# Half of the k tiles of the gate and up products as seven products of sums, four of them in turn in one bank

## The reference

```python
m = rms_norm(h, ffn_norm_g)
return h + (jax.nn.silu(m @ w_gate) * (m @ w_up)) @ w_down
```

## Time and profile before

| what | value |
|---|---|
| time, median of 3 | 2576.79 us (2575.72 to 2576.93) |
| the profiled execution's own time | 2576.22 us |
| its span | 2574.4 us |
| TensorE busy | 2561.0 us (99%) |
| VectorE, ScalarE, GpSimd busy | 1603.7, 1473.3, 824.6 us |
| granted TensorE clock | 1.00 |
| read from HBM | 487.38 MB |

### The profile page before, as it was taken

One profiled execution on the slowest core, in us unless ns is written; L12 is line 12 of the kernel. 1 busy time (PEld: TensorE's weight loads), 2 busy tenths in 40 slices (PEclk: granted clock), 3 DMA queues, 4 the chain that ended last, 5 costly groups with the idle time before them and its releaser, 6 DMA issues.

```text
span 2574.4 us, 30659 instructions
## 1 busy us (share of the span) xinstructions
PE 2561.0 (99%) x11740; PEld 2122.9 (82%) x11740; DVE 1603.7 (62%) x1799; ACT 1473.3 (57%) x1811; POOL 824.6 (32%) x368
## 2 busy tenths in 40 slices
PE   9999999999999999999999999999999999999999
PEld 7888888888887888888888888888878888888887
DVE  6798955434347878787533467456477878786222
ACT  7776645445455656566544575565565656566333
POOL 2687753344441000000444455333320000003443
PEclk9999999999999999999999999999999999999999
DMA  8766654466666475656566644554557565655554
GB/s 302 222 209 204 178 192 161 162 223 210 204 203 246 168 250 174 243 184 217 190 215 205 223 168 157 172 196 142 185 194 247 174 243 183 234 194 194 202 203 147
DMA packets 174705, 516.13 MB, mean 200 GB/s; under 512 B 108027, under 2 KB 111068, under 8 KB 117216
## 3 DMA queue, kind: packets, MB, share of 16 engines
q1 hardware_dynamic: 174128, 513.64, 59.9%
q10 hardware_dynamic: 432, 0.52, 0.1%
HBM read 487.38 MB, written 2.10 MB: 190 GB/s over the span
## 4 chain that ended last, share of the span: by engine, by line
PE 94%; DVE 2%; issue 1%; ACT 1%; POOL 1%; DMA 0%; SPq 0%; ACTq 0%; DVEq 0%; POOLq 0%
PE PB L858 18%; PE PB L862 18%; PE PB L859 18%; PE PB L925 8%; PE PB L926 8%; PE PB L929 8%; PE PB L909 2%; PE PB L906 2%; PE PB L904 2%; ACT WH L1460 1%; PE PB L1168 1%; PE PB L1010 0%; DVE WL L2251 0%; PE PB L1040 0%; POOL WL L3321 0%
## 5 line engine op out<-in xcount | busy, mean ns | idle before, releaser
L3321 POOL TENSOR_TENSOR WL<-RAW,WH 128x1024 fp32r<-128x1024 f32 x280 | 703.1, 2512 | 1730.0 <-ACT WH L1460 1729.1
L1460 ACT ACTIVATE WH<-RAW 128x1024 fp32r<-128x1024 f32 x738 | 776.2, 1057 | 797.6 <-PE PB L862 634.3
L2251 DVE TENSOR_TENSOR WL<-RAW,WH 128x1024 fp32r<-128x1024 f32 x456 | 613.6, 1348 | 753.6 <-ACT WH L1460 752.3
L858 PE MATMUL PB<-WH,HNH 128*128 128x512 f32 x1152 | 458.6, 398 | 2.6 <-ACT TM L2036 2.4
L862 PE MATMUL PB<-WL,HNH 128*128 128x512 f32 x1152 | 449.4, 390 | 1.5 <-POOL WL L3321 1.5
L859 PE MATMUL PB<-WH,HNL 128*128 128x512 f32 x1152 | 448.6, 389 | 0.0
L858 PE MATMUL PB<-WH,HDH 128*128 128x512 f32 x704 | 273.9, 389 | 0.0
L859 PE MATMUL PB<-WH,HDL 128*128 128x512 f32 x704 | 273.9, 389 | 0.0
L862 PE MATMUL PB<-WL,HDH 128*128 128x512 f32 x704 | 273.9, 389 | 0.0
L858 PEld LDWEIGHTS PB<-WH,HNH 128*128 128x128 f32 x1152 | 216.4, 188 | 50.5 <-ACT TM L2036 3.2
L862 PEld LDWEIGHTS PB<-WL,HNH 128*128 128x128 f32 x1152 | 216.2, 188 | 49.0 <-POOL WL L3321 3.4
(11 more groups left out here) (450 smaller groups left out, 3887.0 us busy)
## 6 DMA issues: line engine op xcount, KB each, us to landing
RAW<-in_w_gu SPq DMA_DIRECT2D x136, 1024.0 KB, 7.2
RAW<-in_w_dn SPq DMA_DIRECT2D x88, 1024.0 KB, 4.8
RAW<-in_w_in_a SPq DMA_DIRECT2D x53, 1024.0 KB, 5.2
RAW<-in_w_in SPq DMA_DIRECT2D x45, 1024.0 KB, 4.8
RAWX<-in_w_gu SPq DMA_DIRECT2D x40, 1024.0 KB, 6.6
RAW<-in_w_out SPq DMA_DIRECT2D x32, 1024.0 KB, 4.7
RAW<-in_w_ga SPq DMA_DIRECT2D x24, 1024.0 KB, 4.8
RAW<-in_w_gb SPq DMA_DIRECT2D x24, 1024.0 KB, 4.8
```

The source lines that it names most:

```text
L858: e.matmul(o, hi[:, k, x], WH[:, s, c], start=k == 0, stop=False)
L1460: e.activation(wh(key), source(key), ACT.Copy).then_inc(*wt.act.mark(("wh", *key)))
L2251: e.tensor_tensor(to, raw, hi, ALU.subtract).then_inc(*wt.dve.mark(("wl", *key)))
L3321: e.tensor_tensor(to, raw, hi, ALU.subtract).then_inc(*wt.pool.mark(("wl", *key)))
```

## The change

- Quarters 0 and 1 of the k tiles are done as seven products of sums in all groups 1 to 10, quarters 2 and 3 plainly. A group has 7 x 2 x 2 x 3 = 84 and 96 matmuls, 180 in all.
- A unit of weights is now a key pair (block, c), c being one of its halves, in the order b11, b22, t1, t2, b21, t3, up 2, t4, gate 2, gate 3, up 3.
- Four blocks (b11, t2, t3, t4) and the second token half of the gate columns are summed in one bank x. ScalarE copies what x holds after b11, t2 and t3 (`part`, at k == 10, 36, 53), and t1 from bank z (k == 28). A block that goes on in x waits for the copy. Odd and even groups use two sets of four banks.
- The first sum, t1 = gate 0 + up 0, is made by a DMA issued by GpSimd that reads gate 0 from HBM again and adds it into the buffer that holds up 0 (`first_sum`). It waits for the load of up 0. The sums t2, t3 and t4 stay with VectorE, now for both halves.
- There are five buffers for loads in the gate and up part. To make room, X (2 MB) is stored to HBM early in group 0 and brought back (`x_back`) at the start of the down products.
- The loads of a group come in the order up 0, gate 0, up 1, gate 1, up 2, gate 2, gate 3, up 3.

```diff
-BLOCKS = ("b11", "b21", "b22", "t1", "t2", "t3", "t4")
-BANK_OF = (1, 2, 3, 5, 6, 7, 4)
-SUMMED = (1,)
-FIRST_PLAIN = 0
-SUM_BEHIND = {0: 3, 2: 4, 3: 5, 4: 6}
-STARTS = {(32 * i + 6) // 7: i for i in range(7)}
+BLOCKS = ("b11", "b22", "t1", "t2", "b21", "t3", "t4")
+BANK_OF = {"b11": "x", "b22": "y", "t1": "z", "t2": "x", "b21": "w", "t3": "x", "t4": "x"}
+SUM_BEHIND = {("b22", 1): (("t2", 0),), ("t1", 0): (("t2", 1),), ("t1", 1): (("t3", 0),), ("t2", 0): (("t3", 1),),
+              ("b21", 0): (("t4", 0),), ("b21", 1): (("t4", 1),)}
...
+        AWAY = nc.dram_tensor("away", (128, 2, 2048), F32).ap()
...
+        RAWX = [ar(f"RAWX{i}", [128, RU * 128], 16 + 8 * i) for i in range(2)]
+        WX = [at(f"WX{i}", [128, 2, SU * 128], F32R, (arena + 32 * KB, xt_off, xt_off + 8 * KB)[i]) for i in range(MORE)]
+        CP = ar("CP", [128, 2, 512], 40)
...
+        items = [(b, c) for b in BLOCKS[:6] for c in range(2)] + [(("up", 2), c) for c in range(2)]
+        items += [("t4", c) for c in range(2)] + [((of, d), c) for of, d in (("gate", 2), ("gate", 3), ("up", 3)) for c in range(2)]
+        takes = [6 if b in BLOCKS else 12 for b, c in items]
+        starts = [-(-128 * sum(takes[:i]) // sum(takes)) for i in range(len(items))]
+        place_in_group = [("up", 0), ("gate", 0), ("up", 1), ("gate", 1), ("up", 2), ("gate", 2), ("gate", 3), ("up", 3)]
...
+            if place >= NRAW and raw_before[n] < n - 50:
+                first_in_raw[n] = NT["wo" if wider[n][0] == 1 else "mn"] + 7
             loaded[place] = n, loaded[place][1] + 1
             raw_place[n], raw_count[n] = place, loaded[place][1]
-            raw_due.setdefault(16 * (n - (5 if n in wider else 4)) + 1, []).append(n)
+            raw_due.setdefault(16 * (n - (6 if n in wider else 4)) + 1, []).append(n)
...
+            if j % 2:
+                return {"x": PB[3], "y": mb(nt), "z": mb(nt + 1), "w": mb(nt + 2)}
+            return {"x": PB[4], "y": PB[5], "z": PB[6], "w": PB[7]}
...
+                elif p in wider and wider[p][3] < 2:
+                    stage, j, of, d = wider[p]
+                    e.wait_ge(*low_half(stage, j, {("up", 0): "t1", ("gate", 0): "t3", ("up", 1): "t2", ("gate", 1): "t4"}[of, d], 1))
+                    if of == "up":
+                        e.wait_ge(*wt.dve.done("sum", stage, j, ("t4" if d else "t2"), 1))
...
+                        if j == 0 and k == 50:
+                            for h in range(2):
+                                e.wait_ge(*m.dve.done("x", before, 3, h))
+                            e.dma_start(AWAY[:, :, :], X[:, :, :]).then_inc(landed["x away"], 16)
...
+            def x_back(stage):
+                e.wait_ge(*wt.pe.done("nt", NT[{1: "gu1", 3: "gu2"}[stage]] + 43))
+                e.dma_start(X[:, :, :], AWAY[:, :, :]).then_inc(landed["x back"], 16)
...
+                def of_sums(block, c):
+                    key, q = (stage, j, block, c), BANK_OF[block]
+                    begins = c == 0 and block in ("b11", "b22", "t1", "b21")
+                    if begins:
+                        bank_free(q)
+                    if j == 1 and block == "b22" and c == 0:
+                        e.wait_ge(*m.act.done("sums", stage))
+                        e.wait_ge(*m.dve.done("sums", stage))
+                    if c == 0 and block in ("t2", "t3", "t4"):
+                        e.wait_ge(*m.act.done("part", stage, j, {"t2": "b11", "t3": "t2", "t4": "t3"}[block]))
+                    e.wait_ge(*wt.act.done("wh", *key))
+                    for r in range(2):
+                        t = three(banks[q], left(block, 2 * c + r), key, slice(r * 512, (r + 1) * 512), begins and r == 0,
+                                  c == r == 1 and block in ("b11", "t1", "t2", "t3"), r == 0, block in ("t2", "t3", "t4"))
+                    t.then_inc(*wt.pe.mark(("unit", *key)))
...
+                def part(j, block, to, *before):
+
+                    banks = banks_summed(j, NT[gu] + 4)
+                    e.wait_ge(*wt.pe.done("unit", stage, j, block, 1))
+                    if before:
+                        e.wait_ge(*before)
+                    e.activation(to, banks[BANK_OF[block]][:, :], ACT.Copy).then_inc(*m.act.mark(("part", stage, j, block)))
...
+                        if k == 10:
+                            part(j, "b11", CP[:, 0, :], *(m.dve.done("taken", stage, j - 1, "w") if j > 1 else ()))
                         if k == 16:
                             hidden_split(j - 1)
-                        if k == 50:
-                            e.wait_ge(*wt.pe.done("unit", stage, j, SUMMED[-1], 0))
-                            e.wait_ge(*m.act.done("planes", "z", stage, j - 1, 1))
-                            e.activation(SIG[:, 0, :], PB[3][:, :], ACT.Copy).then_inc(*m.act.mark(("taken", stage, j, 1)))
+                        if k == 28:
+                            part(j, "t1", flat(ST[:, :, :]), *(m.dve.done("taken", stage, j - 1, "y") if j > 1 else ()))
+                        if k == 36:
+                            part(j, "t2", CP[:, 1, :], *(m.dve.done("taken", stage, j - 1, "z") if j > 1 else ()))
+                        if k == 53:
+                            part(j, "t3", CP[:, 1, :], *m.dve.done("u4", stage, j))
                         if k in (74, 82):
                             hidden_joined(j - 1, (k - 74) // 8)
-                        if k in (117, 119):
-                            h = (k - 117) // 2
-                            e.wait_ge(*m.dve.done("taken", stage, j, (2, 4)[h]))
-                            e.activation(SIG[:, h, :], SIG[:, h, :], ACT.Silu, scale=RTOK[:, h:h + 1]).then_inc(
-                                *m.act.mark(("silu", stage, j, h)))
+                        if k == 113:
+                            e.wait_ge(*wt.pe.done("product", stage, j, "x"))
+                            e.wait_ge(*m.act.done("planes", "z", stage, j - 1, 1))
+                            e.activation(SIG[:, 1, :], banks_summed(j, NT[gu] + 4)["x"][:, :], ACT.Silu, scale=RTOK[:, 1:2]).then_inc(
+                                *m.act.mark(("silu", stage, j, 1)))
+                        if k == 116:
+                            e.wait_ge(*m.dve.done("taken", stage, j, "w"))
+                            e.activation(SIG[:, 0, :], SIG[:, 0, :], ACT.Silu, scale=RTOK[:, 0:1]).then_inc(
+                                *m.act.mark(("silu", stage, j, 0)))
...
+                if block == "t2":
+                    e.wait_ge(*low_half(*s, "b22", c))
+                    e.wait_ge(*t1_is_there(*s))
+                    e.tensor_tensor(t2, t1, t2, ALU.add).then_inc(*wt.dve.mark(("sum", *s, block, c)))
+                if block == "t3":
+                    e.wait_ge(*low_half(*s, "b11", c))
+                    e.wait_ge(*wt.dve.done("sum", *s, "t2", c))
+                    e.tensor_tensor(b11, t2, b11, ALU.subtract).then_inc(*wt.dve.mark(("sum", *s, block, c)))
+                if block == "t4":
+                    e.wait_ge(*low_half(*s, "b21", c))
+                    e.wait_ge(*wt.dve.done("sum", *s, "t2", c))
+                    e.tensor_tensor(b21, t2, b21, ALU.add).then_inc(*wt.dve.mark(("sum", *s, block, c)))
...
+                def first_columns(j):
+
+                    e.wait_ge(*wt.pe.done("product", stage, j, "w"))
+                    e.wait_ge(*m.act.done("part", stage, j, "b11"))
+                    e.wait_ge(*m.act.done("planes", "z", stage, j - 1, 1))
+                    e.tensor_tensor(SIG[:, 0, :], CP[:, 0, :], banks_summed(j, NT[gu] + 4)["w"][:, :], ALU.add).then_inc(
+                        *m.dve.mark(("taken", stage, j, "w"), *([("free", NT[gu] + 42)] if j == 9 else [])))
+
+                def less_u2(j):
+
+                    e.wait_ge(*m.act.done("part", stage, j, "t1"))
+                    e.wait_ge(*m.act.done("part", stage, j, "t2"))
+                    u4 = flat(ST[:, :, :])
+                    e.tensor_tensor(u4, u4, CP[:, 1, :], ALU.subtract).then_inc(*m.dve.mark(("u4", stage, j)))
+
+                def up_columns(j):
+
+                    banks, u4 = banks_summed(j, NT[gu] + 4), flat(ST[:, :, :])
+                    e.wait_ge(*wt.pe.done("product", stage, j, "y"))
+                    e.wait_ge(*m.dve.done("u4", stage, j))
+                    e.tensor_tensor(u4, banks["y"][:, :], u4, ALU.add).then_inc(
+                        *m.dve.mark(("y", stage, j), *([("free", NT[gu] + 43)] if j == 9 else [])))
+                    e.wait_ge(*wt.pe.done("product", stage, j, "z"))
+                    e.wait_ge(*m.act.done("part", stage, j, "t3"))
+                    e.tensor_tensor(CP[:, 1, :], banks["z"][:, :], CP[:, 1, :], ALU.subtract).then_inc(
+                        *m.dve.mark(("z sum", stage, j), *([("free", NT[gu] + 41)] if j == 9 else [])))
                     for h in range(2):
                         e.wait_ge(*m.act.done("silu", stage, j, h))
-                        e.wait_ge(*m.dve.done("taken", stage, j, (3, 8)[h]))
```

(30 more changed lines are left out.)

281 lines of the change are left out of this document (103 added, 178 removed).

## The result

| | before | after |
|---|---|---|
| time, median | 2576.86 us | 2693.24 us (2689.66 to 2694.31) |
| ratio | 1 | 1.045, 95% from 1.0432 to 1.0468 |
| profiled execution: time, span | 2576.22, 2574.4 us | 2694.31, 2692.5 us |
| granted TensorE clock | 1.00 | 0.986 |
| distance of the pairs of transposes | 42.15 us | 47.9 us |

The account below looks back on a forecast made before the run. TensorE, busy 99% of the span, was taken to bound the kernel; after the change a ring of waits through the load buffers: 2576.2 - 27.2 + 18 x (43.5 - 40.8) = 2597.6 us, range 2551 to 2655.

Parts of the forecast that it names:

- 120 matmuls fewer: On TensorE, 6 of 186 matmuls gone in each of 2 x 10 groups, at 0.2266 us: 27.2 us less.
- VectorE's 35.5 us in a group: Low halves, sums and work at the banks on VectorE: 35.5 us of a group's 40.8, so it fits.
- The ring as what decides: Waits from group to group through load buffers, SyncE's queue and gate 0: 41.2 us, 43.5 with the accumulate, against TensorE's 40.8.
- the steps to the load and to the transposes: Last low half to the load's issue, 1.3 us; that load's issue to that of the transposes, 0.45.
- the landing of gate 0: Load of gate 0 behind the transposes: lands 5.0 to 6.5 us after its issue, 5.3 in the middle.
- The second path: From a group's end on TensorE to the copy of x ahead of t3: 13.8 us against TensorE's 13.6, no slack.
- The price of the accumulate: What gate 0 loses to the accumulating DMA crossing beside it: 2.3 us taken, bounds 0 and 4.6; called the weakest term.
- the upper bound of 4.6: Most that gate 0 could lose, in us, if the accumulate counts as two loads and all goes ahead.
- Two of my signs: Accumulate landing 8 to 12 us after issue; ScalarE's longest wait in a group ahead of b11's first split, for gate 0.
- The hold of the transposes: On SyncE's queue, two transposes with one load just ahead hold it for 4.93 us; 7 would make the forecast wrong.
- The first groups: Wait at the first group's bank, 2.1 us in both stages together, may go: between 0 and -2, taken as 0.
- The one with two loads: Rival: accumulate counts as two loads or slower, gate 0 loses 4.6: 45.8 us, 2639; landing 3 us later, 2693. Chance 0.17.

Follow-up runs that it names:

- experiment 3: Against the changed kernel, the same DMA from the same queue copies gate 0 without the add; 2637.11 us (one run).
- experiments 4: Against the changed kernel, the first sum t1 is made by VectorE in two halves, with no accumulating DMA; 2637.41 us (one run).
- experiment 6: Against the changed kernel, transposes at the group's start (k == 0) and first sum by VectorE, no accumulating DMA; 2565.64 us, 0.9963 of the kernel before.
- experiment 5: Against the changed kernel, the transposes stand at the group's start (k == 0), ahead of gate 3, accumulate kept; 2616.00 us, 1.0152 of the kernel before.
- experiment 2: Against the changed kernel, the accumulating DMA and the sum t1 are left out, so t1 is up 0 alone; 2592.39 us (one run).

## Why the prediction was wrong

**Right.** 120 matmuls fewer at 0.2266 us. VectorE's 35.5 us in a group. The ring as what decides. Of its path, VectorE's work, the copy between the splits and the steps to the load and to the transposes were right to 0.3 us together (34.26 - 4.25 = 30.0 for 29.75), and the landing of gate 0 to half a us (5.8 for 5.3). Only at the loads did the ring take another way, through up 1. The second path, seen in every experiment. And the sign.

**The price of the accumulate was the step that failed.** I took 2.3 us, "the share of one load, since it writes as much as one", put on gate 0. It costs 5.1 us of all engines and not 2.5, as experiment 3 shows, and it hit not gate 0, which lost 0.3 us, but up 1, which lost about 5: 2.5 + 2.5 + 5.1 = 10.1 us of engine time stand ahead of the moment at which all three are there, and up 1 landed 12.6 us after its issue. 4.25 us in the ring. Without it the kernel is 101 us faster. The rule on the add was in the working and pointed to the upper bound of 4.6. Against it I had weighed the Trainium skill's page "DMA: Bandwidth & Descriptors", section "Queues, rings and completion order", by which an engine takes packets from its queues in turn. My reading of it, that gate 0 waits for as much of the other queue as it has itself, did not come true: 0.3 us and not 2.3. Why gate 0 loses so little wasn't tried. What two queues owe is paid by someone, here by the load behind. Two of my signs told it: the accumulate landed 12.4 to 14.6 us after its issue and not 8 to 12, and in the group shown ScalarE's longest wait was 4.42 us in front of up 1, against 2.11 in front of gate 0. I asked what the transfer takes from the next load and not when the last of all that cross must be there.

**The hold of the transposes was the second.** 4.93 us for "one load just ahead", measured 5.5 to 8.3. The rows to know better were there: in the trace before, the pairs between two groups were held for 7.1 to 8.8 us, the longest shown in the earlier trace rows, all with two loads just ahead; the 4.93 came from the down part, where loads are issued further apart. I counted the loads issued within half a microsecond, but gate 3 and up 3, issued 4.5 to 5 us earlier, were most likely still crossing; no view shows that directly. The sentence "if the transposes hold the queue for 7 us and not for 5: then the ring is 2 longer whatever the accumulate does" was right to the size: the 18 holds have a mean of 6.8 us, 1.9 more.

**The first groups were not looked at.** I had the accumulate start when up 0 has landed. In the first group with sums it stands in GpSimd's queue behind low halves of the plain group and starts 13.8 us after that; VectorE waits 8.6 us for it, TensorE 7.5 and 6.9 us in the two stages, and 2.3 more at half clock. I counted 0 to -2 there. It is 16.9 us, and experiments 4 and 6, which have no accumulate, are at 1.1 a stage again.

**What each is worth.** Of the 96 us between forecast and result, in round numbers: 18 x (4.25 - 2.3) = 35 for the accumulate in the ring, 18 x 1.9 = 34 for the hold, 17 for the first groups, and the last 9 are 18 x 0.5, the part of the ring that these don't cover; gate 0 landed in 5.8 us on the mean and not in 5.3.

**The rivals.** The one with two loads had the right price, and its last half-sentence, "if it lands 3 us later than that, 2693", the measured time; it had 0.17. That the time is the same is luck: it is a ring of 48.8 with nothing at the first groups, and measured were 47.9 and 16.9 us there. It put the price on gate 0 or on t2, where it was on up 1, and the hold, which gives the other 2 us, it did not have. The range ended at 2655 because it left out just this tail. By the ring with both sizes right, 41.2 + 1.9 + 4.25 = 47.4, the sum would have been 2549.0 + 18 x 6.55 = 2667, and with the first groups 2684.

**Open.** In four of the eight distances that follow the first group of the first stage TensorE's granted clock fell to 1.2 GHz for about seven matmuls after a wait of 3.1 us. These four are 48.3 us on the mean and the other four 47.5. Why in these and not in the others wasn't tried. Nor did I try an order of the copies of x that would shorten the second path, the 0.6 us a group that experiment 6 still waits.

## What to carry to other kernels

Where work is taken from the engine that bounds, look for the ring: from the giving up of a buffer through the load, the queue and the splits back to the same buffer, and put every transfer of the group on it with the time at which the last that cross together must be there. A DMA that adds cost two loads here, and a transfer that waits for the one before it has two landings in a row; a sum on an engine with idle time can be cheaper than a DMA that is "free". DMA transposes did best where nothing was under way ahead of them in their queue (2.60 us of hold for 5.5 to 8.3), and a hold that costs nothing today is a debt that the next change to the kernel has to pay.

## What the runs showed of the hardware

- A pair of DMA transposes held the queue that issued it for 2.60 us when no load had been issued for 7 us (experiment 5; 3.4 to 3.7 once in each stage), for 4.9 to 5.4 with one load just ahead, and for 5.5 to 8.3 in the changed kernel, with one just ahead and two more issued 4.5 to 5 us earlier.
- A DMA of 1 MB that adds into the buffer took 5.1 us of all sixteen engines, the same without the add 2.5. It landed 12.4 to 14.6 us after its issue in the changed kernel, 9.1 to 11.2 when it started after up 1 had landed, and without the add in 6.1 to 11.2.
- An accumulate issued from another queue 0.3 us behind a load took 0.3 us from that load and about 5 from the one behind it (12.5 to 13.0 us to landing for 7.0 to 8.4).
- After 7.5 us of idle time TensorE ran at half clock for 5 us; after 3.1 us for 3 us in four groups of eight; in experiment 2 also after 1.95 us (half clock from 980.6 to 983.8).
- The DMA share of a stretch can read over 1 (1.04 at 287 GB/s, 1.19 at 213 in the kernel before), and a share of 0.98 came with 407 GB/s: it tells the time in which engines had packets, not the rate.
